# 32 bytes of room behind each chunk of two operands of TensorE in a two-block network

## What is computed

```python
def mlstm_layer(h, w_in, ...):                    # h (1, 256, 1024), w_in (1024, 4096)
    xm, z = jnp.split(h @ w_in, 2, axis=-1)
    ...

def swiglu_ffn(h, w_in, w_out):                   # w_in (1024, 5632), w_out (2816, 1024)
    gate, up = jnp.split(h @ w_in, 2, axis=-1)
    return (jax.nn.silu(gate) * up) @ w_out

for l in range(DEPTH):                            # DEPTH = 2: four feed-forwards in all
    x = x + FFN_RESID * swiglu_ffn(rms_norm(x, ffn1_norm[l]), ffn1_w_in[l], ffn1_w_out[l])
    ...
    x = x + FFN_RESID * swiglu_ffn(rms_norm(x, ffn2_norm[l]), ffn2_w_in[l], ffn2_w_out[l])
```

## The kernel before

| operand | bytes from one chunk to the next | start, rest by 512 |
|---|---|---|
| `x_hi`, `x_lo`, `sq_lo` | 1024 | 128 |
| `wi_hi`, `wi_lo` | 512 | 192 |
| `wx_hi`, `wx_lo` | 512 | 0 |
| `wm_hi`, `wm_lo` | 512 | 96 |
| `y_hi`, `y_lo` | 1024 | 0 |
| `w_hi`, `w_lo` | 512 | 0 |
| `h_split` | 2048 | 0 |
| `hid_hi`, `hid_lo` | 512 (tiles of 128 tokens) | 0 |

## Time and profile before

### The profile page before, as it was taken

How to read it: one execution, slowest core, us unless ns; L and a number is a source line. 1 busy time by engine, 2 the same in 40 slices (tenths; PEclk the granted TensorE clock), 3 DMA queues, 4 the chain that set the end, 5 groups by cost and what they waited for, 6 DMA issues and landing times.

```text
span 2376.0 us, 33274 instructions
## 1 busy us (share of the span) xinstructions
PE 2259.9 (95%) x12878; PEld 1731.4 (73%) x12878; DVE 1252.6 (53%) x2287; ACT 948.1 (40%) x1699; POOL 113.8 (5%) x96
## 2 busy tenths in 40 slices
PE   5999999998999899889999999999999999999999
PEld 3877784543577444468888689888788896798887
DVE  4624544111323411167755566777677636666776
ACT  2532212110322311164544664645554446655543
POOL 1000000000000000000024200000000052000000
PEclk9999999999999999999999999999999999999999
DMA  9976469999713899956654325466566535154663
GB/s 356 318 234 235 159 253 382 429 429 423 277 71 123 374 429 429 419 180 190 193 173 160 107 88 188 140 206 185 159 193 193 183 109 177 47 198 120 204 186 96
DMA packets 310253, 535.63 MB, mean 225 GB/s; under 512 B 14894, under 2 KB 200944, under 8 KB 296304
## 3 DMA queue, kind: packets, MB, share of 16 engines
q1 hardware_dynamic: 309180, 532.61, 62.2%
q10 hardware_dynamic: 948, 1.28, 0.2%
HBM read 532.81 MB, written 1.05 MB: 225 GB/s over the span
## 4 chain that ended last, share of the span: by engine, by line
PE 85%; DVE 7%; ACT 3%; issue 2%; DMA 2%; SPq 1%; POOL 0%; POOLq 0%; ACTq 0%; DVEq 0%
PE bank L601 15%; PE bank L1070 14%; PE bank L892 13%; PE yacc L930 9%; PE bank L897 7%; PE bank L585 5%; PE yacc L807 2%; PE yacc L618 2%; PE bank L636 2%; PE bank L1010 1%; PE bank L1285 1%; PE yacc L1082 1%; PE bank L672 1%; PE yacc L1229 1%; PE bank L766 1%
## 5 line engine op out<-in xcount | busy, mean ns | idle before, releaser
L1453 ACT ACTIVATE arena<-bank 128x256 f32<-128x256 f32 (+3 forms) x382 | 146.6, 407 | 575.3 <-PE bank L601 122.4
L892 PE MATMUL bank<-h_split,w_hi 128*128 128x512 f32 x1408 | 352.1, 392 | 0.0
L2366 DVE TENSOR_TENSOR w_lo<-wring,w_hi 128x1024 fp32r<-128x1024 f32 x264 | 307.5, 1218 | 3.3 <-ACT w_hi L1678 3.3
L1678 ACT ACTIVATE w_hi<-wring 128x1024 fp32r<-128x1024 f32 x264 | 277.6, 1056 | 48.4 <-PE yacc L930 48.2
L892 PEld LDWEIGHTS bank<-h_split,w_hi 128*128 128x128 f32 x1408 | 259.2, 189 | 50.0
L897 PEld LDWEIGHTS bank<-h_split,w_lo 128*128 128x128 f32 x1408 | 193.6, 191 | 20.5 <-issue 4.0
L897 PE MATMUL bank<-h_split,w_lo 128*128 128x256 f32 x1408 | 201.8, 285 | 3.8 <-ACT h_split L1587 3.6
L2976 POOL TENSOR_TENSOR wx_lo<-wring,wx_hi 128x1024 fp32r<-128x1024 f32 x42 | 107.3, 2557 | 1894.7 <-ACT wx_hi L1493 1894.7
L1070 PE MATMUL bank<-wring,arena 128*64 128x512 f32 x768 | 172.3, 603 | 12.2 <-issue 8.3
L1070 PE MATMUL bank<-arena 128*64 128x512 f32 x672 | 168.3, 594 | 10.6 <-issue 7.0
L1690 ACT ACTIVATE H<-bank 128x256 f32<-128x256 f32 x176 | 67.3, 383 | 250.9 <-PE bank L897 250.9
(11 more groups left out here) (412 smaller groups left out, 3793.9 us busy)
## 6 DMA issues: line engine op xcount, KB each, us to landing
wring<-in_ffn_w_in SPq DMA_DIRECT2D x176, 512.0 KB
wring<-in_w_ada SPq DMA_DIRECT2D x24, 2048.0 KB
wring<-in_ffn_w_out SPq DMA_DIRECT2D x88, 512.0 KB
wring<-in_w_in SPq DMA_DIRECT2D x20, 2048.0 KB
wring<-in_moe_w_down SPq DMA_DIRECT2D x16, 2048.0 KB, 23.2
wring<-in_moe_w_gate SPq DMA_DIRECT2D x16, 2048.0 KB, 18.1
wring<-in_moe_w_up SPq DMA_DIRECT2D x16, 2048.0 KB, 22.6
arena<-in_moe_w_gate SPq DMA_DIRECT2D x12, 2048.0 KB, 14.3
```

Source lines behind the costliest of these rows:

```text
L892: return mm(b[:, :], r(w_hi[:, j % 2, g, c * HB:(c + 1) * HB]), r(h_split[:, c, :, :].rearrange("p a t -> p (a t)")), start=start, stop=st ...
L1453: ins = f(dst, bank_of(name)[0:dst.shape[0], 0:T] if src is None else src, func, **kw)
L1678: f(w_hi[:, j % 2, part, :].bitcast(F32R), wring[:, u % WSLOTS, part * DC * HB:(part + 1) * DC * HB], ACT.Copy).then_inc(w_hi_ready[part], 1)
L2366: tt(w_lo[:, j % 2, part, :].bitcast(F32R), wring[:, (u0 + j) % WSLOTS, part * DC * HB:(part + 1) * DC * HB], w_hi[:, j % 2, part, :], ALU ...
```

## The change

Behind each chunk of 128 columns in the buffers of `wi_hi` and `wi_lo` 8 float32 columns (32 bytes) stay unused: the stride from chunk to chunk is 544 bytes instead of 512, and a buffer of 8 chunks has 4352 bytes instead of 4096. Behind each chunk of 512 columns of `h_split` 8 columns stay unused too: the stride is 2080 bytes instead of 2048. Nothing is computed on the unused columns. `wi_hi` starts where it did; `wi_lo` starts 768 bytes later, and `hid_hi`, `hid_lo`, `hid` and `sg`, which lie behind `h_split`, 256 bytes later. The number and the order of the instructions, what each engine waits for and all DMAs are as before. ScalarE and VectorE now write a tile of `wi_hi` or `wi_lo` as 8 pieces of 128 columns, where they wrote 1024 in a row.

```diff
--- before.py
+++ after.py
@@ -201,10 +201,10 @@
             wt_mix = [part(name, [P, 2, DC * P]) for name in ("wx_hi", "wx_lo")]
         with ExitStack() as overlay:
             part("before_w_in", [P, 12336])
-            wt_w_in = [part(name, [P, WBUFS, DC * P]) for name in ("wi_hi", "wi_lo")]
+            wt_w_in = [part(name, [P, WBUFS, DC, P + 8]) for name in ("wi_hi", "wi_lo")]
         w_hi = sb("w_hi", [P, 2, 3, DC * HB])
         w_lo = sb("w_lo", [P, 2, 3, DC * HB])
-        h_split = sb("h_split", [P, DC, 2, T])
+        h_split = sb("h_split", [P, DC, 2 * T + 8])
         hid_hi = sb("hid_hi", [P, 2, T])
         hid_lo = sb("hid_lo", [P, 2, T])
         hid = sb("hid", [P, T])
@@ -416,9 +416,11 @@
 
         def part_tile(lo, phase, q):
 
+            if phase == "w_in":
+                return wt_w_in[lo][:, q % WBUFS, :, 0:P]
             k, cols = split[phase][1][q][2:4]
             n = cols if k == 2 else P
-            w = (wt_w_in if phase == "w_in" else wt_mix if "mix" in phase else wt_merge)[lo]
+            w = (wt_mix if "mix" in phase else wt_merge)[lo]
             return w[:, q % w.shape[1], 0:k * n].rearrange("p (k n) -> p k n", k=k)
 
         def tile_done(phase, q):
@@ -890,11 +892,11 @@
 
                         def whole(c, start, stop):
                             return mm(b[:, :], r(w_hi[:, j % 2, g, c * HB:(c + 1) * HB]),
-                                      r(h_split[:, c, :, :].rearrange("p a t -> p (a t)")), start=start, stop=stop,
+                                      r(h_split[:, c, 0:2 * T]), start=start, stop=stop,
                                       skip_group_check=True)
 
                         def left(c, start, stop):
-                            return mm(b[:, 0:T], r(w_lo[:, j % 2, g, c * HB:(c + 1) * HB]), r(h_split[:, c, 0, :]),
+                            return mm(b[:, 0:T], r(w_lo[:, j % 2, g, c * HB:(c + 1) * HB]), r(h_split[:, c, 0:T]),
                                       start=start, stop=stop, skip_group_check=True)
 
                         if fresh:
@@ -1584,7 +1586,7 @@
                         act.wait_ge(normed.sem, normed.upto("act"))
                         offset = lnv[:, 2 * n + 1, k:k + 1] if dst is not X else vec("ln_b", (2 * DEPTH - 1) * DC + k)
                         if dst is X:
-                            f(h_split[:, k, 0, :].bitcast(F32R), X[:, k, :], ACT.Identity, scale=vec("ffn1", k),
+                            f(h_split[:, k, 0:T].bitcast(F32R), X[:, k, :], ACT.Identity, scale=vec("ffn1", k),
                               bias=lnv[:, 0, k:k + 1]).then_inc(h_hi_ready.sem, 1)
                         f(dst[:, k, :], dst[:, k, :], ACT.Identity, bias=offset).then_inc(ready.sem, 1)
                 if tag == "ln00":
@@ -1712,7 +1714,7 @@
                     act.wait_ge(*full(f"{tag}.x{kk}"))
                     for a in range(2):
                         k = 2 * kk + a
-                        f(h_split[:, k, 0, :].bitcast(F32R), bank_of(f"{tag}.x{kk}")[:, a * T:(a + 1) * T], ACT.Copy,
+                        f(h_split[:, k, 0:T].bitcast(F32R), bank_of(f"{tag}.x{kk}")[:, a * T:(a + 1) * T], ACT.Copy,
                           scale=vec(gain, l * DC + k)).then_inc(h_hi_ready.sem, 1)
                 token_scale(phase)
                 high(0, 0, 2)
@@ -2405,7 +2407,7 @@
                     for k in range(DC):
                         dve.wait_ge(h_hi_ready.sem, h_hi_ready.upto("dve"))
                         dve.wait_ge(x_ready.sem, x_ready.upto("dve"))
-                        stt(h_split[:, k, 1, :].bitcast(F32R), X[:, k, :], vec(gain, l * DC + k), h_split[:, k, 0, :],
+                        stt(h_split[:, k, T:2 * T].bitcast(F32R), X[:, k, :], vec(gain, l * DC + k), h_split[:, k, 0:T],
                             ALU.mult, ALU.subtract).then_inc(h_lo_ready.sem, 1)
                     for part in range(2):
                         low(0, 1, part)
@@ -2413,8 +2415,8 @@
                     dve.wait_ge(h_hi_ready.sem, h_hi_ready.upto("dve", 2))
                     for a in range(2):
                         k = 2 * kk + a
-                        last = stt(h_split[:, k, 1, :].bitcast(F32R), bank_of(f"{tag}.x{kk}")[:, a * T:(a + 1) * T],
-                                   vec(gain, l * DC + k), h_split[:, k, 0, :], ALU.mult, ALU.subtract)
+                        last = stt(h_split[:, k, T:2 * T].bitcast(F32R), bank_of(f"{tag}.x{kk}")[:, a * T:(a + 1) * T],
+                                   vec(gain, l * DC + k), h_split[:, k, 0:T], ALU.mult, ALU.subtract)
                     moved(f"{tag}.x{kk}", last)
                 token_rstd()
                 for j in range(2 if tag == "f10" else early, 2):
```

## The result

| | kernel before | changed kernel |
|---|---|---|
| median, lowest to highest run, us | 2379.75, 2378.47 to 2380.09 (4 runs) | 2386.20, 2385.00 to 2390.77 (4 runs) |
| span of the profiled execution, us | 2376.0 | 2383.2 |

The changed kernel takes 1.0035 times as long, with a 95% interval of 1.0023 to 1.0047: slower, and the whole interval lies past the 0.2% that can be told from no change. The medians lie 6.45 us apart, 0.27%; the ratio is estimated from all runs and not from the two medians.

What follows compares the result with a forecast made beforehand. TensorE, busy 95% of the span, was taken as the bound, by the pace of matmul behind matmul. Terms -2.9 + 2.3 + 0 + 0.9 = +0.3 us on the 2376.0 span gave a median of 2380.0, range 2365 to 2390.

Steps and rivals of the forecast that it cites:

- third rival: Changing differences let neither L892 nor the first projection settle into their quick pace: +9.0 us, 2388.7; chance 0.25.
- L892: Feed-forward, 512-wide matmuls: mean of 226.3, 230 and 233.1, 229.8 ns, +2.3 us; bounds -2.6 to +7.0.
- L897: Feed-forward, 256-wide matmuls: 116.7 instead of 118.75 ns, -2.9 us; at best -7.7, no loss.
- L930: Feed-forward, 12 matmuls of down per step, strides kept: taken as 0; bounds 0 to -3.0 us.
- The first projection: Six pieces of L601: 116.7 instead of 115.1 ns, +0.9 us; bounds -0.9 to +2.0; what follows 122 us hidden.
- The writers: ScalarE and VectorE writing wi_hi and wi_lo tiles, and the features: smaller pieces cost nothing, 0.
- the addresses don't matter: Rival for all matmuls: widths and what ran before set the pace; 2379.7 us; no effect had chance 0.15.
- the weighed rule: Skill's rule of two independent TensorE read ports: operands' relative place can't matter, all terms zero, 2379.7 us.
- the equal rest is what costs: Equal low-address bits slow feed-forward matmuls; the room ends it, first projection quicker too: -14.2 us, 2365.5; chance 0.28.
- My picture: Matmul pace: two SBUF readers get in each other's way, with a state carried from matmul to matmul; inferred, unsized.

Runs made afterwards that it cites:

- walk_together: Kernel before, with 32 bytes of room behind each chunk of both feed-forward operands, features starting 32 bytes further, down weights unchanged: 2379.77 us, ratio 1.0003.
- starts_even: Kernel before, no room; h_split starts 0, 64, 128, 192 bytes later in the four feed-forwards, first-projection weights 32 bytes later every four tiles: 2381.88 us, one execution.
- shift_together: Kernel before, with everything from the arena on 64 bytes later (x_hi, x_lo, sq_lo stay), so all feed-forward operands move together: 2386.88 us, ratio 1.0032.
- shift_parts: Kernel before, with x_hi, x_lo, sq_lo, y_hi, y_lo shifted so L601 and L1082 have difference 192: 2375.11 us, ratio 0.9976; repeated 2376.01 us, 0.9986.
- shift_all: Kernel before, with the shifts of shift_parts plus w_lo's two L897 parts 64 bytes later: 2378.89 us, ratio 0.9993; repeated 2380.05 us, 1.0001.
- room_256: Kernel before, with 256 bytes of room behind each chunk of h_split instead of the change's 32, none in the weights: 2378.82 us, ratio 1.0000.

## Why the prediction was right and wrong

The forecast was 2380.0 in a range of 2365 to 2390, and no measurable change as the likeliest outcome. The range holds 2386.2, but the time lies 6.2 us above the forecast, and the change is measurable. It came out near the size of the third rival, the walk breaks a rhythm that is good now, to which I gave 0.25: 9.0 us there, against 6.45 between the medians and 7.2 between the spans. Its reason holds in part, as told below. Term by term:

- **L892, the term that failed.** I took the mean of three rows, 229.8 ns, for seven differences, of which the rows showed only one at 512 columns, L618's, and wrote +2.3 us. Measured: 233.6 and 233.9 ns, (7.0 + 3.8) ns x 704 = +7.6 us, past even the upper bound of 7.0 that I drew from L618. The table says why a mean was the wrong guess: two of my three rows, 226.3 and 230, were the same difference of 0, and the third was the only evidence on all others. L618's 233.1 ns at 224 stood for the crowd: the feed-forward has 233.6 and 232.8 there, with the operands the other way round, which I had held against that row. I had the right price in the bounds and chose against the one row that spoke for the new layout.
- **L897.** Forecast -2.9 us from 116.7 ns; measured 118.6 instead of 119.0 ns, -0.6 us. The five rows that I averaged lie at differences of 192, 128, 32 and 160, with 192 in twice; over all eight the table has 118.0. And a walk doesn't average the fixed runs in a plain way, as walk_together shows.
- **L930.** Forecast 0; measured 228.4 instead of 229.0 ns, -0.6 us.
- **The first projection.** Forecast +0.9 on the six pieces, measured +1.8, near the upper bound of +2.0: 65.34 us for 552 matmuls, 118.4 ns each instead of 116.7. It had been at 192, the best difference, mostly at its quick pace of 113.3 ns; with the walk it is at 117.5 within every group of 96. What comes behind 122 us wasn't hidden altogether: the whole stage grew by 2.2.
- **The writers.** Forecast nothing, measured -3 and -2 ns each: right.
- **The sum.** 7.6 - 0.6 - 0.6 + 2.2 = +8.6 us from the paces; the spans differ by 7.2 and the medians by 6.45. The stage cut gives 5.8 for the feed-forwards where the paces give 6.4. The way up to the first projection was 1.1 shorter in the profiled execution; over the profiles of this case that way varies from 37.8 to 40.5 us.

**The rivals.** That the addresses don't matter is refuted by starts_even: the same instructions at 226.6 or 233.4 ns, by 192 bytes of offset alone. The time that I gave for the weighed rule, no change, is refuted with it. The Trainium skill ("TensorE: Matmul & The Clock Gate", Part 2, step by step) says that loading the next tile's weights takes no SBUF read bandwidth from the running matmul; here what counts is where these two reads lie against each other, up to 8 ns in 227, and moving both leaves the pace as it was (shift_together), though no run shows what inside the chip makes it so. That the equal rest is what costs is half true: at 256 columns 0 is among the slow differences. But leaving it by a walk gains next to nothing (0.4 ns), only going to 192 gained more, and at 512 columns 0 is the best. That a changing difference breaks a rhythm, the third rival, gives the right size, but for the most part by luck: a difference that stays fixed is nearly as slow, unless it is 0 or, behind a 256-wide group, 64. The change from chunk to chunk adds 1.2 of the 7.0 ns and 1.6 of the 3.8. That moving on has a price of its own shows in walk_together, where the difference stays 0.

**My picture** of two readers in each other's way with a state carried along holds for what it was read from: the pace depends on the difference, and on the neighbours (L892 at 226.6 or 230.1 ns, L897 at 192 at 114 to 115 or at 117.8), though for L897 no run shows that it is the neighbours. It was too coarse to price a new layout.

## What to carry to other kernels

When a product is bounded by matmul behind matmul, measure its pace at a few fixed offsets of one operand against the other before changing strides: a start is moved with one line, and here offsets were worth up to 4% of a matmul, in different directions for 512 and 256 columns. For float32r operands as here, the pace was best with the moving and the next stationary chunk at the same start by 256 bytes for 512 columns, with the moving one 192 bytes further for 256 columns, and with strides that are multiples of 256. Check it in the chain and in the time: at 192 a run can also fall to the slow pace, and of the versions that used this, shift_parts gained 3.3 and 4.9 us and shift_all nothing that could be measured. And where a forecast lacks the row for the new state, the row of the operation that is already in such a state weighs more than a mean of rows that are not.

## What the runs showed of the hardware

- The pace of float32r matmuls depends on how the two operands lie in SBUF: 226.6 to 234.8 ns at 512 columns and 113.3 to 120.4 ns at 256, at the same granted clock of 1.00. A difference of 256 bytes is as good as one of 0 (room_256), and moving both by 64 bytes changes nothing in the feed-forward (shift_together).
- At 512 columns a matmul comes 226 to 227 ns after the one before it, or some ns later, up to 239. At a difference of 0 the delay dies out: behind the 256-wide group, `down` in the kernel before has 233 236 228 233 231 226 ns and then stays at 226 to 227. In the changed kernel it dies out in `down`, which didn't move, in the same way (238 232 231 227), and never in L894.
- Equal differences are not enough. With both operands walking by 32 bytes, every second matmul is 10 ns late. And at a difference of 192 runs of 256-wide matmuls have two steady paces, 113.3 and 117.8 ns, with the same addresses: in the pieces of the first projection, and in shift_parts_2 one merge each. A run keeps its pace for up to a whole merge. What carries this from group to group stays open.
- Executions of one kernel differ by several us in the mixers: the second mixer stage of shift_parts took 267.0 and 260.9 us in two of them, with both second merges at 129.6 us and the granted clock at 0.91 and 0.95 from 1900 to 1970 us. The two paces at 192 add up to 3.2 us per merge. That is as much as all the gains here, so a layout is better judged by the pieces of the chain than by one span.
